# Latent attention scores: from two f32 products to five products of rounded halves

## The reference, cut to what matters

```
q  = rmsnorm(cq) @ w_uq      # per head 128 nope + 64 rotary numbers, the latter rotated
kn = rmsnorm(ckv) @ w_ukv    # per head 128 nope keys, 128 values
kpe = rotate(h @ w_in[kpe])  # 64 rotary keys, for all heads
s = (q_nope . kn + q_rope . kpe) / sqrt(192)
o = softmax(s) @ v           # per 128 queries
```

## Time and profile before

| what | value |
|---|---|
| median of 3 runs | 2625.49 us (2623.31 to 2629.7) |
| the profiled execution, its own time | 2628.0 us |
| its span, first to last instruction | 2626.2 us |
| PE busy over the span | 2489.8 us, 95% |
| DVE, ACT, POOL busy | 51%, 30%, 34% |
| the latent attention's set-up on PE | 2023 to 2065 us |
| the latent attention's 16 units | 2065 to 2167 us |

### The profile page before, as it was taken

How to read it: one execution, slowest core, us unless ns; L and a number is a source line. 1 busy time by engine, 2 the same in 40 slices (tenths; PEclk the granted TensorE clock), 3 DMA queues, 4 the chain that set the end, 5 groups by cost and what they waited for, 6 DMA issues and landing times.

```text
span 2626.2 us, 30806 instructions
## 1 busy us (share of the span) xinstructions
PE 2489.8 (95%) x13049; PEld 2036.1 (78%) x13049; DVE 1327.1 (51%) x1704; ACT 795.3 (30%) x1083; POOL 882.9 (34%) x633
## 2 busy tenths in 40 slices
PE   7999899999999999898999999989999889999998
PEld 4888778788888888687777778868887337788886
DVE  2998764645444444866566645564642223311113
ACT  2323652211111112326532222244433233322223
POOL 2006002233233342462044545535433002444442
PEclk9998999899999999899999999989999998999999
DMA  8223103224343332221044554522104001232331
GB/s 267 92 97 98 49 1 113 81 81 129 121 137 93 117 117 68 73 91 56 1 136 132 155 180 146 157 72 62 36 17 128 0 1 48 73 105 87 98 95 58
DMA packets 309225, 240.57 MB, mean 92 GB/s; under 512 B 10692, under 2 KB 304831, under 8 KB 309087
## 3 DMA queue, kind: packets, MB, share of 16 engines
q1 hardware_dynamic: 308674, 238.47, 29.8%
q10 hardware_dynamic: 414, 0.13, 0.0%
HBM read 232.29 MB, written 2.10 MB: 89 GB/s over the span
## 4 chain that ended last, share of the span: by engine, by line
PE 86%; DVE 9%; ACT 3%; DMA 1%; issue 1%; POOL 0%; SPq 0%; DVEq 0%; ACTq 0%
PE ps L2493 61%; PE ps L1148 5%; PE ps L721 2%; DVE mod_w L2125 2%; PE ps L2528 2%; PE ps L934 2%; PE ps L672 2%; DVE mod_ctx L2125 2%; PE ps L1168 1%; PE ps L2408 1%; PE ps L2445 1%; PE ps L748 1%; PE ps L1191 1%; DVE small L1038 1%; PE ps L896 1%
## 5 line engine op out<-in xcount | busy, mean ns | idle before, releaser
L1631 POOL TENSOR_TENSOR w_lo<-raw,w_hi 128x512 fp32r<-128x512 f32 x518 | 757.1, 1491 | 1413.9 <-ACT w_hi L1739 1413.9
L2493 PE MATMUL ps<-h_hi,w_hi 128*128 128x512 f32 x1994 | 651.1, 373 | 25.4 <-DVE h_lo L2089 21.3
L2493 PE MATMUL ps<-h_lo,w_hi 128*128 128x512 f32 x1994 | 641.1, 367 | 0.0
L2493 PE MATMUL ps<-h_hi,w_lo 128*128 128x512 f32 x1994 | 640.0, 367 | 0.0
L1739 ACT ACTIVATE w_hi<-raw 128x2048 fp32r<-128x2048 f32 (+2 forms) x155 | 264.8, 1709 | 600.5 <-PE ps L2493 374.5
L2493 PEld LDWEIGHTS ps<-h_hi,w_hi 128*128 128x128 f32 x1994 | 341.3, 191 | 94.3 <-issue 23.3
L2493 PEld LDWEIGHTS ps<-h_lo,w_hi 128*128 128x128 f32 x1994 | 341.6, 191 | 66.0 <-issue 0.2
L2493 PEld LDWEIGHTS ps<-h_hi,w_lo 128*128 128x128 f32 x1994 | 340.7, 191 | 67.0
L2016 ACT ACTIVATE xg<-ps 128x512 f32<-128x512 f32 (+1 forms) x66 | 44.2, 670 | 677.8 <-PE ps L2493 491.4
L2125 DVE SCALAR_TENSOR_TENSOR mod_w<-mod_w,cond 128x512 f32<-128x512 f32 x224 | 242.0, 1080 | 3.4
L2493 PE MATMUL ps<-hid_hi,w_hi 128*128 128x512 f32 x704 | 232.2, 370 | 0.0
(11 more groups left out here) (364 smaller groups left out, 3240.6 us busy)
## 6 DMA issues: line engine op xcount, KB each, us to landing
mod_w<-in_w_mod SPq DMA_DIRECT2D x72, 1024.0 KB, 9.5
raw<-in_w_ffn_in SPq DMA_DIRECT2D x88, 512.0 KB, 5.2
raw<-in_w_in SPq DMA_DIRECT2D x54, 512.0 KB, 4.8
raw<-in_w_ffn_out SPq DMA_DIRECT2D x48, 384.0 KB, 3.8
raw<-in_w_out SPq DMA_DIRECT2D x24, 512.0 KB, 4.5
raw<-in_w_gate SPq DMA_DIRECT2D x22, 512.0 KB, 4.1
raw<-in_w_up SPq DMA_DIRECT2D x22, 512.0 KB, 5.4
raw<-in_w_down SPq DMA_DIRECT2D x24, 384.0 KB, 3.7
```

The lines of the kernel that those rows point to most:

```text
L1631: ins = pool.tensor_tensor(w_lo[:, s, at:end], raw[:, s, at:end], w_hi[:, s, at:end].bitcast(F32), ALU.subtract)
L2493: ins = pe.matmul(ps[0:m, at:at + tw], weight(part, k, cols), v[:, held[k] if held else k, t0:t0 + tw], start=(at_k == 0 and j == 0 and no ...
```

## The change

The scores of a unit are now five F32R products instead of two F32 ones. Nope: hi·hi, hi·lo and lo·hi over 128 rows each. Rotary: a head's tile `q_turn` holds the rounded query in the 64 rows of the head's parity and the remainder in the other 64, so that one product over all 128 rows against `kpe_hi` (which stands in both halves) gives hi·hi + lo·hi; a fifth product over the head's own 64 rows adds hi·lo with `kpe_lo`. For this ACT's copies of queries and keys out of PSUM write the rounded halves, with five further ACT copies (one of `kpe`, four of 64 rows of the rotated queries), and DVE gets 13 subtractions: four for the low queries (from PSUM), one for `kpe_lo`, four of 64 rows for the rotary remainders, four for the low keys (from PSUM). PE gets two kinds of added waits, on `l_low`, ahead of overwriting the PSUM banks that DVE now reads too. The low queries live in a part of `x` that the recurrence used as scratch, `q_turn` in a part of `f_back`.

```diff
-            k_nope = sb("k_nope", [P, HEADS, TOK], F32, s)
-            q_nope = sb("q_nope", [P, HEADS, LAT], F32, s)
-            q_rope = sb("q_rope", [P, 2, LAT], F32, s)
+            kn_hi = sb("kn_hi", [P, HEADS, TOK], F32R, s)
+            kn_lo = sb("kn_lo", [P, HEADS, TOK], F32R, s)
...
@@ last_layer_pe
             pe.wait_ge(l_taken, HEADS)
+            pe.wait_ge(l_low, HEADS)
...
                 pe.wait_ge(l_taken, 7 + t)
+                if t < HEADS:
+                    pe.wait_ge(l_low, 9 + t + 1)
...
-                return [(q_nope[:, u["h"], u["q"]:u["q"] + P], lambda k0, kw: k_nope[:, u["h"], k0:k0 + kw]),
-                        (q_rope[half, u["h"] // 2, u["q"]:u["q"] + P], lambda k0, kw: kpe[half, k0:k0 + kw])]
+                return [(high, lambda k0, kw: kn_hi[:, h, k0:k0 + kw]),
+                        (high, lambda k0, kw: kn_lo[:, h, k0:k0 + kw]),
+                        (low, lambda k0, kw: kn_hi[:, h, k0:k0 + kw]),
+                        (q_turn[:, h, q:q + P], lambda k0, kw: kpe_hi[:, k0:k0 + kw]),
+                        (q_turn[half, h, q:q + P], lambda k0, kw: kpe_lo[half, k0:k0 + kw])]
@@ last_layer_act
+            act.wait_ge(l_norm, 3)
+            act.activation(kpe_hi[:, :], kpe[:, :], ACT.Copy).then_inc(l_high, 1)
+            for h in range(HEADS):
+                own = slice(64 * (h % 2), 64 * (h % 2) + 64)
+                if h % 2 == 0:
+                    act.wait_ge(l_turned, h // 2 + 1)
+                act.activation(q_turn[own, h, :], q_rope[own, h // 2, :], ACT.Copy).then_inc(l_high, 1)
@@ last_layer_dve
             spread(dve, l_root, n_root[:, 4:10], TOK // P).then_inc(l_spread, 1)
+            for h in range(HEADS):
+                dve.wait_ge(l_taken, h + 1)
+                dve.scalar_tensor_tensor(qn_lo(h), halves(ps[:, Q_AT[h]:Q_AT[h] + LAT]), q_scale,
+                                         halves(qn_hi[:, h, :].bitcast(F32)), ALU.mult, ALU.subtract).then_inc(l_low, 1)
             dve.wait_ge(l_wide, 1)
...
+            dve.wait_ge(l_high, 1)
+            dve.tensor_tensor(kpe_lo[:, :], kpe[:, :], kpe_hi[:, :].bitcast(F32), ALU.subtract).then_inc(l_low, 1)
+            for h in range(HEADS):
+                own, other = (slice(64 * side, 64 * side + 64) for side in (h % 2, 1 - h % 2))
+                dve.wait_ge(l_high, 2 + h)
+                dve.tensor_tensor(q_turn[other, h, :], q_rope[own, h // 2, :], q_turn[own, h, :].bitcast(F32), ALU.subtract
+                                  ).then_inc(l_low, 1)
+            for h in range(HEADS):
+                dve.wait_ge(l_taken, 7 + h)
+                dve.tensor_tensor(kn_lo[:, h, :], ps[:, 1024 * h:1024 * h + TOK], kn_hi[:, h, :].bitcast(F32), ALU.subtract
+                                  ).then_inc(l_low, 1)
```

More of the change, by code:

```diff
@@ L227, in program @@
         sums_eps = sb("sums_eps", [P, HEADS * TOK // P])
+        with ExitStack() as s:
+            x_turn = sb("x_turn", [P, KD, TOK], F32R, s)
         x = sb("x", [P, KD, TOK])
@@ L237, in program @@
         with ExitStack() as s:
+            qn_hi = sb("qn_hi", [P, HEADS, LAT], F32R, s)
+            kpe_hi = sb("kpe_hi", [P, TOK], F32R, s)
+            kpe_lo = sb("kpe_lo", [P, TOK], F32R, s)
+        with ExitStack() as s:
             g_high = sb("g_high", [P, 3584], F32, s)
@@ L294, in program @@
             hg = sb("hg", [P, HEADS, LAT], F32, s)
+            with ExitStack() as s2:
+                q_turn = sb("q_turn", [P, HEADS, LAT], F32R, s2)
             f_back = sb("f_back", [P, HEADS * TOK], F32, s)
@@ L310, in program @@
         w_uq = f_back[:, 0:1536].rearrange("p (k n) -> p k n", k=2)
+        q_rope = f_back[:, 2048:3072].rearrange("p (j t) -> p j t", j=2)
         mix_out = f_back[:, 1536:2560].rearrange("p (s t) -> p s t", s=2)
@@ L322, in spare_x, with qn_lo @@
             return x[:, 2 * k:2 * k + 2, LAT:TOK]
+        def qn_lo(h):
+            return x_turn[:, 2 * h:2 * h + 2, LAT:TOK]
         def halves(part):
@@ L393, in program @@
                                                               sem("g_am"), sem("g_s"), sem("g_o"), sem("g_saved"))
+        l_high, l_low = sem("l_high"), sem("l_low")
         l_sq, l_ss, l_std, l_norm, l_swap, l_up, l_taken, l_turned = (
@@ L1308, in scores @@
             def scores(u, c):
-                half = slice(64 * (u["h"] % 2), 64 * (u["h"] % 2) + 64)
-                return [(q_nope[:, u["h"], u["q"]:u["q"] + P], lambda k0, kw: k_nope[:, u["h"], k0:k0 + kw]),
-                        (q_rope[half, u["h"] // 2, u["q"]:u["q"] + P], lambda k0, kw: kpe[half, k0:k0 + kw])]
+                h, q = u["h"], u["q"]
+                half = slice(64 * (h % 2), 64 * (h % 2) + 64)
+                high = qn_hi[:, h, q:q + P]
+                low = qn_lo(h)[:, q // CTX, q % CTX:q % CTX + P]
+                return [(high, lambda k0, kw: kn_hi[:, h, k0:k0 + kw]),
[3 more added lines that the diff above has]
+                        (q_turn[half, h, q:q + P], lambda k0, kw: kpe_lo[half, k0:k0 + kw])]
             attention_pe(pe, 2, scores, lambda kt, h: v_l[:, kt, h * P:h * P + P])
@@ L1436, in last_layer_act @@
                 act.wait_ge(l_up, h + 1)
-                act.activation(q_nope[:, h, :], ps[:, Q_AT[h]:Q_AT[h] + LAT], ACT.Copy, scale=q_scale).then_inc(l_taken, 1)
+                act.activation(qn_hi[:, h, :], ps[:, Q_AT[h]:Q_AT[h] + LAT], ACT.Copy, scale=q_scale).then_inc(l_taken, 1)
             for j in range(2):
@@ L1440, in last_layer_act @@
                 act.activation(q_rope[:, j, :], ps[:, ROPE_AT[j]:ROPE_AT[j] + LAT], ACT.Copy, scale=q_scale).then_inc(l_taken, 1)
+            act.wait_ge(l_norm, 3)
[5 more added lines that the diff above has]
+                act.activation(q_turn[own, h, :], q_rope[own, h // 2, :], ACT.Copy).then_inc(l_high, 1)
             for h in range(HEADS):
                 act.wait_ge(l_up, 9 + h)
-                act.activation(k_nope[:, h, :], ps[:, 1024 * h:1024 * h + TOK], ACT.Copy).then_inc(l_taken, 1)
+                act.activation(kn_hi[:, h, :], ps[:, 1024 * h:1024 * h + TOK], ACT.Copy).then_inc(l_taken, 1)
             for t in range(TOK // P):
```

## The result

The changed kernel took 2609.85 us, the median of 7 runs (2606.68 to 2613.44), the kernel before 2625.68 (7 runs beside them); the ratio is 0.9938, 95% interval 0.9928 to 0.9949, some 16 us. A second measurement gave 2611.62 against 2623.42, a ratio of 0.9949 (0.9936 to 0.9962), some 13 us by the ratio and 11.8 between the medians. Forecast were 2613 us (2603 to 2620) and 12.5 us gained. The profiled execution took 2609.85 us, its span 2608.0 against 2626.2.

What follows compares the result with a forecast made beforehand. TensorE was taken to bound the attention units; scores 0.83 us shorter in 15 counted units give 12.5 us, set-up 0. From the profiled 2628.0 that makes 2615.5, as a median 2613 us, range 2603 to 2620.

Steps and rivals of the forecast that it cites:

- The scores: TensorE's score products in each attention unit: 3.17 us falls to 2.34, 0.83 less, and the unit's period follows to 3.90.
- The change of rows: Switching between 64-row and 128-row operands among F32R score products: 0 to 0.4 us each, 0.20 taken, three staying per unit.
- The cheap change: Rival: row changes between F32R score products cost little, at most 21.5 us gained, 2604 to 2610; chance 0.17.
- the 0.10 seen in the earlier trace: Delay between F32R products where 64 rows give way to 128: start 0.21 us later instead of 0.113.
- The start: First units: first transposes wait for the first scaling, PE idles some 0.8 us, so 15 x 0.83 counts.
- The set-up at nothing: Work ahead of the units: added ACT copies and 10.3 us of DVE subtractions fall into idle time, cost 0.
- the rotation that it was to leave alone: Set-up on DVE: key latents' scaling starts some 0.7 us late, absorbed by 2.98 us of idle time ahead of L1571.
- No gain: Rival: ten weight loads show in the scores (2631, half price 8 us shorter), or set-up subtractions reach the path (2623); chance 0.15.
- The clock: Rival: TensorE's clock falls in the units, doubling PE's parts, 57 us more, 2683; chance 0.06.
- the slower case: The outcome in which TensorE's clock falls during the units: 2683 us, chance 0.06.
- The total: Whole kernel: 12.5 us gained, a median of 2613 us; 9 to 15 us gained had chance 0.62.

Runs made afterwards that it cites:

- two kernels that take changes out: Changed kernel with its 64-row products last (2604.75 us, 0.9937 to before), and with its fifth product over all 128 rows (2601.82 us, 0.9921; again 0.9901).
- the set-up alone: Changed kernel with its whole new set-up, but scores again as two F32 products a piece: 2625.61 us, ratio to before 1.0011.
- one product a piece: Changed kernel with one F32R product of high nope halves for each column piece, the other four left out: 2600.88 us, ratio to before 0.9914.

## Why the prediction was right

*The scores* are the step that carried it: 2.34 us worked out, 2.35 in the chain; 3.90 a unit, 3.91 measured; 12.5 us in all, 12.4 measured in the units. *The change of rows* was its unknown, 0 to 0.4 with 0.20 taken; two kernels that take changes out measure 0.2 each. The rule of the Trainium skill (TensorEngine Tiling (Array Packing), Key Properties), that a change of tiling mode drains the engine, spoke for keeping the 0.2, and the two kernels agree with it as far as a price of 0.2 for every change goes. The cheap change, a rival at 2604, is refuted by the same two kernels; the 0.10 seen in the earlier trace rows was only a part of the price. One remark of the prediction does not follow from its own figures: the columns' cost is not halved, it goes from 2.52 to 1.74 us, a third less; no term of the sum used it.

*The start* went as put: one of the first two scores counts, and the first transposes wait for the first scaling. *The set-up at nothing* held as far as the profiles show: the set-up alone returns before's units and no gain, and twice the subtractions fit. In the changed kernel's timeline the last low query, the rotation that it was to leave alone, and the last low key:

```profile
2028.69 0.69 DVE L1594 SCALAR_TENSOR_TENSOR x_turn<-ps,qn_hi 128x512 fp32r<-128x512 f32 x1 [1.02 <-ACT qn_hi L1459]
...
2033.51 0.96 DVE L1604 TENSOR_TENSOR l_tmp<-ps,rot 128x768 f32<-128x768 f32 x1 [2.40 <-PE ps L1293]
...
2051.85 0.96 DVE L1625 TENSOR_TENSOR kn_lo<-ps,kn_hi 128x768 fp32r<-128x768 f32 x1 [1.62 <-ACT kn_hi L1472]
```

DVE's idle time ahead of the rotation went from 2.98 us to 2.40 and still ends on PE, and the last subtraction, at the 0.96 that was taken, ends 1 us behind ACT's last copy, as put. *No gain* through ten weight loads falls by the 0.23 and 0.11 between products.

*The clock* did not fall in the changed kernel (1.00 over its units), so the slower case did not come. Its mechanism is real, though: with one product a piece the clock stood at 0.76.

*The total* came out 3 us better than said, 2609.85 for 2613, and in the second timing 1.4. That is no step of the sum: the profiles place it in stretches that hold the same work in both kernels and that vary between executions of one kernel. Whether 1 to 2 us of it are the change's after all is open.

## What to carry to other kernels

Count a product's price by passes over the columns and by changes between 64-row and 128-row operands, not by rows: half the rows cost as much as all. Where a 64-row product stands among 128-row ones, fill the rows (here both halves of a split operand against the same keys) or at least put the 64-row products together. In the units the first was worth 10 us more and the second 5.6, where the whole change was worth 12.4. A change of 10 us in 2600 is settled by the length of its own stretch in the profile, since the totals here lay up to 3 or 4 us off what that stretch says, in either direction.

## What the runs showed of the hardware that was not expected

Taking work from TensorE can lengthen the work that is left to it: scores of two products a unit instead of ten left the granted clock at 0.76 instead of 1.00, values products at 6.64 to 7.89 us instead of 5.42, and the units only 1.4 us shorter than with all ten. And the same program shows, from one execution to the next, a mean clock of 0.80 or 0.90 in the same 33 us, for 2.6 us more or less.
